# Ranking two of eight expert heads between the next stage's dot products instead of inside the query stage

## Chip, cores and metric

The kernel runs on one NeuronCore of a Trainium2 chip. The metric is the device time of one execution in microseconds (us); three runs of each kernel are timed.

## What is computed

One step of a one-layer decoder for a prompt of 512 tokens and a sample group of 8 x 8 tokens: a Mamba-2 branch, a sparse-attention branch, their merge, an output projection, and then a retrieval layer, which the change is about:

```python
def _peer(h, peer_wq, peer_sub_keys, peer_u, peer_v):
    n = h.shape[0]
    q = (h @ peer_wq).reshape(n, PEER_HEADS, 2, PEER_HALF)
    s = jnp.einsum('nhcd,hckd->nhck', q, peer_sub_keys).astype(jnp.float32)
    top_s, top_i = lax.top_k(s, PEER_TOPK)
    cand_s = (top_s[:, :, 0, :, None] + top_s[:, :, 1, None, :]).reshape(n, PEER_HEADS, -1)
    cand_i = (top_i[:, :, 0, :, None] * PEER_KEYS + top_i[:, :, 1, None, :]).reshape(n, PEER_HEADS, -1)
    best_s, best_pos = lax.top_k(cand_s, PEER_TOPK)
    experts = jnp.take_along_axis(cand_i, best_pos, axis=-1)
    g = jax.nn.softmax(best_s, axis=-1)
    act = jax.nn.gelu(jnp.einsum('nd,nhkd->nhk', h, peer_u[experts]).astype(jnp.float32))
    return jnp.einsum('nhk,nhkd->nd', (g * act).astype(peer_v.dtype), peer_v[experts])
```

There are 8 heads with 16 experts each, so every token picks 128 rows of peer_u and 128 rows of peer_v, 4 KB each, out of tables of 16,384 rows.

## The kernel before

The tokens are in five tiles: 0 to 3 are the prompt (128 tokens each), 4 is the sample group. The layer's first part runs in two groups: group a is tiles 0 and 1, group b is tiles 2 and 3 with the sample tokens. Each group goes through the stages conv, ssd, zgate, branch (one block together), kv, qk, cmp_prompt, attn_prompt, merge, out and query. Then come the sample group's own stages: sample_state, mix, branch, cmp, attn, branch, out and query, and at last `rest`.

The retrieval itself (class `Experts`) is laid through all stages from group b's conv on. `lay_out` writes one order of 1,152 **places**: a place "u" is one gather of 128 rows of peer_u (512 KB, an indirect DMA issued by GpSimd, `gather`) and the dot product on VectorE that uses them (`dot_u`), a place "v" is one gather of peer_v, and every four of them a sum on TensorE (`sum_v`). Tile 0's u places are 0 to 127, tile 1's begin at 128, tile 2's at 448. The gathers land in a ring of 14 slots (`NR`; one more from the state stage on). A gather waits until the slot's last reader is done, so it can be only some 14 places ahead of the dots. Each stage has a share of places (`k.share`: conv 60, ssd 28, zgate 56, branch 46, kv 22, qk 30, cmp_prompt 10, attn_prompt 100, ..., query 46, state 112) and calls `ex.dve(i)`, `ex.act(i)`, `ex.pe(i)`, `ex.pool(i)` at fixed points of its own program; each call emits what is due up to place `lo(i + 1)`. All engines work in program order, so an emitted step that waits holds up the stage's own work behind it on that engine.

A tile's experts must be named before its u gathers. **Ranking a head** takes three steps of VectorE: the 16 best of both score halves (`rank_halves`, `top16`), the 16 best of their 256 sums (`rank_sums`), and the experts' numbers (`mark_places`, then `name_marked` on GpSimd, inside the query stage; `name_experts`, all on VectorE, elsewhere). The query stage (`stage_query`) multiplies out scores for its group's two tiles and ranks all 8 heads of the first (tile 0 or 2) itself; at its end VectorE and ScalarE form the softmax (`shift_best`, Exp, `share_best`) and ScalarE copies names and weights (`stage_routes`), and the stage's barrier waits for that. The second tile's scores are stored to memory, and its heads are ranked between the dots of later stages: `load_scores` on GpSimd fetches one head's scores (128 KB), `rank_scores`, `rank_sums` and `name_head` run on VectorE at the 1st, 4th and 7th place after the head's start, `index_head` on ScalarE. The starts are in `rank_place`: for tile 1 places 20 + 30h, for tile 3 places 448 + 20 + 9h.

In group a's query stage ScalarE and TensorE also turn the next group's input (`Ahead`: `turn` is eight transposes of one tile, `spread` eight copies), after the loop over the 16 score halves. The state stage begins on GpSimd with masks and products of its own (L2129 to L2145), ahead of `ex.pool(0)`; on VectorE with `ex.dve(0)`, `ex.dve(1)`, and then the first update of a state (L2223), which waits for TensorE (L2173).

Of the kernel before, what the change touches and what calls it, by code (L numbers as in the profile page):

```python
# [6 lines left out]
F32 = mybir.dt.float32  # L7
# [1890 lines left out]
def stage_query(nc, k, g, following):  # L1898

    with ExitStack() as ctx:  # L1900
# [8 lines left out]
        (sk_in, projected, q_copied, scored, s_copied, ranked, own_s, shifted, exped, routed) = (  # L1909
            sem(n) for n in ("sk_in", "projected", "q_copied", "scored", "s_copied", "ranked", "own", "shifted", "exped",  # L1910
                             "routed"))
# [4 lines left out]
        ex = k.ex  # L1916
        ex.plan(HOOKS, k.share["query"])
# [5 lines left out]
        def _(sp):  # L1923
            def store(i):
                sp.wait_ge(s_copied, i + 1)
                sp.dma_start(k.scores_dram[t0][:, i, :], s[:, i % NS_BUF, 1, :]).then_inc(s_out[i % NS_BUF], 16)
# [5 lines left out]
            for i in range(NS_BUF):  # L1932
                sp.wait_ge(s_out[i], 16 * (HC // NS_BUF))

        @block.gpsimd
        def _(pool):
            own = Link(pool, pool_s)
            for i in range(HOOKS):
# [3 lines left out]
                if i >= 4 and i % 2 == 0:  # L1942
                    h = (i - 4) // 2
# [8 lines left out]
        def _(pe):  # L1952
# [21 lines left out]
            for i in range(HC + 1):  # L1974
# [5 lines left out]
                if i:  # L1980
                    score(i - 1)
            ex.pe(HC + 1)
            ex.pe(HC + 2)
            if ahead:
                for i in range(len(following.tiles)):
                    ahead.turn(i)

        @block.scalar
        def _(act):
# [28 lines left out]
            if ahead:  # L2018
                for i in range(len(following.tiles)):
                    ahead.spread(i)  # L2020
            ex.act(HC + 1)
            act.wait_ge(shifted, 1)
            a.activation(k.best[:], k.best[:], ACT.Exp).then_inc(exped, 1)
            ex.act(HC + 2)
            act.wait_ge(routed, 1)
            act.wait_ge(named, PH)
            ex.stage_routes(t0)
            act.wait_ge(ex.staged, t0 + 1)

        @block.vector  # L2030
        def _(dve):
            v = nc.vector
            own = Link(dve, own_s)
            for i in range(HC + 2):
# [7 lines left out]
                if i >= 2 and i % 2 == 0:  # L2042
                    h = i // 2 - 1
# [8 lines left out]
                if i >= 3 and i % 2 == 1:  # L2052
                    h = (i - 3) // 2
                    rank_sums(v, own, k, h)
                    mark_places(v, own, k, hit[:, h % 2]).then_inc(marked, 1)
            shift_best(v, own, k).then_inc(shifted, 1)
            dve.wait_ge(exped, 1)
            share_best(v, own, k).then_inc(routed, 1)
# [3 lines left out]
        if following:  # L2062
            k.w.start(following)

            @block.sync
            def _(sp):
                sp.wait_ge(projected, HC)
                k.w.feed(sp)

# [1265 lines left out]
class Experts:  # L3335
# [10 lines left out]
    indexed = [0, 2, S]  # L3346

    def __init__(self, nc, k, ctx, looped):
        self.nc, self.k, self.looped = nc, k, looped
# [903 lines left out]
```

## Time and profile before

| | us |
|---|---|
| median of 3 runs | 2729.2 (2728.67 to 2739.69) |
| the profiled execution | 2731.53 |
| its span in the profile | 2729.7 |
| busy: TensorE, VectorE, ScalarE, GpSimd | 2018.4, 1456.9, 673.6, 1478.6 |
| group a's query stage | 585.4 to 669.4 |
| group b's query stage | 1499.9 to 1610.6 |
| sample_state | 1610.6 to 1807.8 |

In rows of the profile PE is TensorE (PEld its weight loads), DVE VectorE, ACT ScalarE, POOL GpSimd and SP the engine that only issues DMAs. `a <- b` names what an instruction writes and reads; `[x <- y]` is idle time x of the engine before it, ended by y. The DMA share is the mean busy share of the core's 16 DMA engines. A dot is one `CUSTOM_DVE_ANT_0` of L3768, 1.22 us long, and the next starts 1.15 us after it.

### The profile page before, as it was taken

Reading aid. Unit: us, or ns where it says so; the run is one execution under the profiler, and the core shown is the slowest. Engines: PE = TensorE matmul, PEld = TensorE weight load, DVE = VectorE, ACT = ScalarE, POOL = GpSimd, SP = SyncE. Lnnn points to the kernel's source line nnn. Section 1 sums busy time; section 2 is a strip of 40 time slices with the busy share of each in tenths; the row PEclk is TensorE's granted clock in tenths of the full one; section 3 lists DMA queues with packets and bytes.
Section 4 is the critical chain, followed back from the end, with each engine's and each line's share of the span. In section 5 each row is a group of like instructions: output and inputs, shape, how many; then the busy total and the mean of one; then the engine's idle time right before and its main releaser. Section 6 shows DMA issues by size and latency. Waiting matters only on the chain. (4 is left out here: it accounts for less than half of the span.)

```text
span 2729.7 us, 31629 instructions
## 1 busy us (share of the span) xinstructions
PE 2018.4 (74%) x10995; PEld 1286.9 (47%) x10995; DVE 1456.9 (53%) x3506; ACT 673.6 (25%) x2035; POOL 1478.6 (54%) x1493
## 2 busy tenths in 40 slices
PE   8999989987977979989988946755267776655044
PEld 6888875655655656654444722322144443111010
DVE  3331013226897975457731568778686665106910
ACT  4441016313547320015531112321011110001000
POOL 1120000006556766656654777787867777567775
PEclk9899989988988999989989967886588987868577
DMA  5414344344895899889889979999999999999998
GB/s 181 169 62 140 129 179 186 134 164 168 302 345 190 323 391 400 326 339 331 333 328 398 347 250 374 411 394 341 398 343 412 409 411 402 402 401 402 409 409 326
DMA packets 209780, 843.32 MB, mean 309 GB/s; under 512 B 25752, under 2 KB 32728, under 8 KB 190104
## 3 DMA queue, kind: packets, MB, share of 16 engines
q0 software_dynamic: 170912, 644.95, 61.8%
q1 hardware_dynamic: 38712, 196.36, 19.3%
q8 instruction: 89, 1.46, 0.2%
q14 instruction: 67, 0.55, 0.1%
HBM read 821.80 MB, written 23.54 MB: 310 GB/s over the span
## 5 line engine op out<-in xcount | busy, mean ns | idle before, releaser
L3604 POOL DMA_INDIRECT e_ring<-in_peer_u,e_idx x523 | 615.2, 1176 | 300.1 <-DVE e_dot L3768 142.7
L3768 DVE CUSTOM_DVE_ANT_0 e_ring<-e_ring,e_h 128x1024 f32<-128x1024 f32 x523 | 631.5, 1243 | 68.7 <-PEq L1159 22.0
L3604 POOL DMA_INDIRECT e_ring<-in_peer_v,e_idxT x487 | 510.7, 1049 | 258.5 <-issue 132.4
L3671 PE MATMUL ps<-e_ring,e_wz 128*32 128x512 f32 x1948 | 316.8, 698 | 261.9 <-DMA e_ring<-in_peer_v,e_idxT 152.9
L3671 PEld LDWEIGHTS ps<-e_ring,e_wz 128*32 128x32 f32 x1948 | 66.9, 119 | 416.7 <-issue 405.5
L363 PE MATMUL ps<-hT_ahead,wb 128*128 128x320 f32 x384 | 110.6, 443 | 0.9 <-DMA wb<-in_weights 0.9
L363 PEld LDWEIGHTS ps<-hT_ahead,wb 128*128 128x128 f32 x384 | 72.9, 195 | 30.1 <-issue 2.7
L1815 POOL CAST ra_atf<-ra_at 128x32 f32<-128x32 uint32 x8 | 1.7, 211 | 149.7 <-DVE ra_hit L1808 149.7
L3812 DVE TENSOR_TENSOR e_x<-e_x,ps 128x512 f32<-128x512 f32 x10 | 6.4, 684 | 141.8 <-PE ps L3671 141.8
L1183 POOL MEMSET inda<- 128x256 f32 x1 | 0.3, 311 | 147.7 <-POOLq L4071 147.7
L3671 PE MATMUL ps<-ring_pair,e_wz 128*32 128x512 f32 x152 | 63.2, 730 | 17.2 <-DMA e_ring<-in_peer_v,e_idxT 11.3
L642 POOL TENSOR_TENSOR sa_xdt<-xnata,dt 128x512 f32<-128x512 f32 x8 | 8.3, 1042 | 116.3 <-ACT hT_ahead L509 99.3
L547 DVE SCALAR_TENSOR_TENSOR ca_acc<-ca_in,vcol,ca_acc 128x256 f32<-128x256 f32 x72 | 34.9, 485 | 61.0 <-ACT ca_acc L492 59.3
L1648 DVE TENSOR_REDUCE apb_nmax<-ps 128x2 f32<-128x768 f32 (+1 forms) x32 | 34.9, 1090 | 47.2 <-PE ps L1540 47.2
L2173 PE MATMUL ps<-ss_bsel,ss_xde 64*128 64x512 f32 x64 | 39.6, 701 | 22.9 <-DVE wb L2223 13.4
L897 PE MATMUL ps<-hT_ahead,wb 128*128 128x320 f32 x192 | 56.0, 446 | 0.0
L547 DVE SCALAR_TENSOR_TENSOR cb_acc<-cb_in,vcol,cb_acc 128x344 f32<-128x344 f32 x72 | 41.7, 579 | 24.3 <-ACT cb_acc L492 22.6
L3671 PE MATMUL ps<-ring_more,e_wz 128*32 128x512 f32 x76 | 45.4, 729 | 7.7 <-DMA e_ring<-in_peer_v,e_idxT 7.7
L363 PE MATMUL ps<-hTa,e_ring 128*128 128x256 f32 x224 | 50.6, 380 | 0.0
L2980 DVE COPY as_pT<-ps 128x512 f32<-128x512 f32 x40 | 26.9, 688 | 43.9 <-PE ps L2849 43.9
L753 ACT ACTIVATE zs<-ps,nacum 128x128 f32<-128x128 f32 x128 | 36.6, 374 | 49.2 <-PE ps L681 49.1
L3039 DVE MAX8 top<-sq_s 128x8 f32<-128x128 f32 x16 | 3.9, 285 | 81.9 <-ACT sq_s L3290 81.5
(778 smaller groups left out, 4610.4 us busy)
## 6 DMA issues: line engine op xcount, KB each, us to landing
wb<-in_weights SPq DMA_DIRECT2D x65, 1024.0 KB, 7.3
e_ring<-in_weights SPq DMA_DIRECT2D x36, 1024.0 KB, 4.9
wb<-in_late_weights SPq DMA_DIRECT2D x6, 2048.0 KB, 10.9
room<-in_late_weights SPq DMA_DIRECT2D x6, 2048.0 KB, 15.7
h<-in_weights SPq DMA_DIRECT2D x10, 1024.0 KB, 8.3
xs<-in_weights SPq DMA_DIRECT2D x9, 1024.0 KB, 7.9
e_ring<-in_peer_u,e_idx POOLq DMA_INDIRECT x523, 8.7
e_ring<-in_peer_v,e_idxT POOLq DMA_INDIRECT x487, 10.6
```

What stands on the lines that cost most here:

```text
L363: last = nc.tensor.matmul(k.ps[:, f % 2, 0:N], w[:, kk, c:c + P], k.hT[:, kk, 0:N], start=(kk == 0), stop=(kk == KD - 1))
L547: last = v.scalar_tensor_tensor(out=dst, in0=src, scalar=wc, in1=dst, op0=ALU.mult, op1=ALU.add)
L642: gp.tensor_tensor(v3(xdt), x3, by_head(k.dt[:, t0 + c, hs], P), ALU.mult).then_inc(xdt_done, 1)
L753: last = a.activation(MT[:, q % 4, j, :], k.ps[:, 1, j * P:j * P + P], ACT.Exp, bias=k.nacum[:, t0 + c, hh:hh + 1])
L897: last = mm(k.ps[:, f % 2, 0:N], w[:, kk, :], k.hT[:, kk, 0:N], start=(kk == 0), stop=(kk == KD - 1))
L1648: v.tensor_reduce(nmax[:, 2 * d:2 * d + 2], k.ps[:, 0:2, 0:width(d)], AX.X, ALU.max, negate=True).then_inc(maxed, 1)
L2173: mm(k.ps[:, 2 + q % 2, :], xde[:, f * P:f * P + P], bsel[:, j % 2, seqs(i), :].rearrange("p b n -> p (b n)"), start=True, stop=True).then ...
L2980: v.tensor_copy(pT[:, 4 * i:4 * i + 4, :], k.ps[:, n % 2, :].rearrange("p (q c) -> p q c", q=4)).then_inc(p_copied, 1)
L3604: nc.gpsimd.indirect_dma_start(out=self.room(place), out_offset=None, in_=k.peer_u if kind == "u" else k.peer_v, in_offset=off).then_inc(s ...
L3671: last = nc.tensor.matmul(k.ps[32 * b:32 * b + 32, self.SUMS + i, :], self.wz[:, at:at + 32], self.room(self.v_at[n])[:, 512 * i:512 * i + ...
L3768: v.tensor_tensor_reduce(uu, uu, self.h[:, tile % 2, :], 1.0, 0.0, ALU.mult, ALU.add, self.dot[:, tile % 2, t:t + 1]).then_inc(self.dotted, 1)
L3812: last = v.tensor_tensor(self.x1[:, c], self.x1[:, c], k.ps[:, self.SUMS + i, :], ALU.add)
```

## The change

Both query stages rank only heads 0 to 5 (`EARLY = 6`) and no longer form the softmax; the barrier waits for the six heads' names alone. Scores of heads 6 and 7 of the first tile are stored too. Those two heads become steps between dots: for tile 0 they start at places 16 and 44, for tile 2 at places 449 and 458. Tile 1's eight heads start at 76, 100, 124, 154, 184, 214, 244 and 274 (from 20, 50, ..., 230), tile 3's at 482 + 9h (from 468 + 9h). The softmax steps follow a tile's last head. The transposes of the next group's input move into the loop. In group a's query stage the wait for the stores comes behind the issue of the next group's first weights.

```diff
@@ class Experts
+    EARLY = 6
+        self.heads = [(t, h) for t in range(S) for h in range(0 if t % 2 else self.EARLY, PH)]
@@ stage_query, SyncE
-                sp.dma_start(k.scores_dram[t0][:, i, :], s[:, i % NS_BUF, 1, :]).then_inc(s_out[i % NS_BUF], 16)
+                sp.dma_start(k.scores_dram[t0 + 1][:, i, :], s[:, i % NS_BUF, 1, :]).then_inc(s_out[i % NS_BUF], 16)
+                if i in left:
+                    sp.dma_start(k.scores_dram[t0][:, i, :], s[:, i % NS_BUF, 0, :]).then_inc(s_out[i % NS_BUF], 16)
@@ stage_query, GpSimd (VectorE alike)
-                if i >= 4 and i % 2 == 0:
-                    h = (i - 4) // 2
+                h = (i - 4) // 2
+                if i % 2 == 0 and 0 <= h < EARLY:
@@ stage_query, TensorE
+                if ahead and 12 <= i < 12 + len(following.tiles):
+                    ahead.turn(i - 12)
             ex.pe(HC + 1)
             ex.pe(HC + 2)
-            if ahead:
-                for i in range(len(following.tiles)):
-                    ahead.turn(i)
@@ stage_query, ScalarE
+                if ahead and 13 <= i < 13 + len(following.tiles):
+                    ahead.spread(i - 13)
             ex.act(HC + 1)
-            act.wait_ge(shifted, 1)
-            a.activation(k.best[:], k.best[:], ACT.Exp).then_inc(exped, 1)
             ex.act(HC + 2)
-            act.wait_ge(routed, 1)
-            act.wait_ge(named, PH)
-            ex.stage_routes(t0)
-            act.wait_ge(ex.staged, t0 + 1)
+            act.wait_ge(named, EARLY)
+            ex.index_rest(t0)
+            act.wait_ge(ex.rest_named, t0 // 2 + 1)
@@ Experts.lay_out
+        for t in range(S):
+            heads = [h for tile, h in self.heads if tile == t]
+            for i, h in enumerate(heads):
+                at = lambda step: self.rank_place(t, i, step)
+                if i >= 2:
+                    load = self.rank_place(t, i - 2, 8)
+                else:
+                    load = 66 + i if t == 1 else self.rank_place(2, i, 8) if t == 3 else self.u_at[P * t]
+                put("pool", load, lambda t=t, h=h: self.load_scores(t, h))
+                put("dve", at(1), lambda t=t, h=h: self.rank_scores(t, h))
+                put("dve", at(4), lambda t=t, h=h: rank_sums(self.nc.vector, self.own, self.k, h))
+                put("dve", at(7), lambda t=t, h=h: self.name_head(h))
+                put("act", at(13 if t < 2 else 9), lambda t=t, h=h: self.index_head(t, h))
...
-    def rank_place(self, t, step):
-        if t == 0 and step >= 0:
-            return 20 + 30 * (step // 9) + step % 9
-        return self.u_at[P * t + 20 + step]
+    def rank_place(self, t, i, step):
+        if t == 0:
+            return 16 + 28 * i + step
+        if t == 1:
+            return 76 + 24 * min(i, 2) + 30 * max(i - 2, 0) + step
+        return self.u_at[P * 2 + (34 if t == 3 else 1) + 9 * i + step]
```

VectorE at the start of the state stage, before: the seventh dot (with the read-out of its sum), the first update, the eighth dot.

```order
L3768 ISA e_ring,e_dot<-e_ring,e_h 128x1024
L3768 ISA e_dot 128x1
L2223 TENSOR_TENSOR wb<-wb,ps 128x512
L3768 ISA e_ring,e_dot<-e_ring,e_h 128x1024
L3768 ISA e_dot 128x1
```

And after the change, from the stage's second dot on (`e_s` is the tile into which a head's scores are loaded):

```order
L3786 ISA e_ring,e_dot<-e_ring,e_h 128x1024
L3786 ISA e_dot 128x1
L3039 MAX top<-e_s 128x8 x2
L3042 MAX_INDEX at<-top,e_s 128x8 x2
L3046 MATCH_REPLACE e_s<-top,e_s 128x128 x2
L3039 MAX top<-e_s 128x8 x2
L3042 MAX_INDEX at<-top,e_s 128x8 x2
L3786 ISA e_ring,e_dot<-e_ring,e_h 128x1024
L3786 ISA e_dot 128x1
```

Seven dots stood ahead of the first update; now two dots, a head's scores, three dots, its sums and two dots do.

GpSimd at the same place, after the change: the last of the stage's own products, then the loads of two heads' scores, then the first gathers. Before, the first gather stood right behind the product.

```order
L2145 TENSOR_TENSOR ss_bsel<-Bs,same 64x1024
L3632 DMA e_s<-scores_scratch 128x256 x2
L3616 DMA ring_more<-in_peer_u,e_idx 128x1024
L3616 DMA e_ring<-in_peer_u,e_idx 128x1024 x7
L3632 DMA e_s<-scores_scratch 128x256
```

So VectorE's third dot of the stage is behind a load that GpSimd issues only after its own products.

VectorE in group b's cmp_prompt stage, after the change: from the stage's first dot to the copy L1455, for which TensorE waits. Before, three dots stood ahead of that copy and nothing else.

```order
L3786 ISA e_ring,e_dot<-e_ring,e_h 128x1024
L3786 ISA e_dot 128x1
L3039 MAX top<-e_s 128x8 x2
L3042 MAX_INDEX at<-top,e_s 128x8 x2
L3046 MATCH_REPLACE e_s<-top,e_s 128x128 x2
L3039 MAX top<-e_s 128x8 x2
L3042 MAX_INDEX at<-top,e_s 128x8 x2
L3786 ISA e_ring,e_dot<-e_ring,e_h 128x1024
L3786 ISA e_dot 128x1
L3786 ISA e_ring,e_dot<-e_ring,e_h 128x1024
L3786 ISA e_dot 128x1
L1455 COPY cpb_pT<-ps 128x256
```

The head's sums now stand ahead of the stage's two copies L1395, and its name behind them at the stage's end.

## Rows read from the trace of the kernel before

**Rows 1.** The page: busy time of each engine; DMA busy tenths in 40 slices
```profile
PE 2018.4 (74%) x10995; PEld 1286.9 (47%) x10995; DVE 1456.9 (53%) x3506; ACT 673.6 (25%) x2035; POOL 1478.6 (54%) x1493
...
DMA  5414344344895899889889979999999999999998
```

**Rows 2.** Windows: length, busy PE, PEld, DVE, ACT, POOL, clock, DMA share, GB/s
```profile
585.40:669.40 84.00, 66.97 (x344) 59.41 (x344) 57.23 (x251) 26.72 (x74) 40.59 (x82) 0.91 0.38 128
...
904.00:988.00 84.00, 78.67 (x317) 53.97 (x316) 77.68 (x162) 23.72 (x72) 68.26 (x50) 0.97 0.96 366
...
1202.40:1224.20 21.80, 15.29 (x80) 10.56 (x80) 14.11 (x46) 3.16 (x6) 11.30 (x13) 0.69 0.86 297
1224.20:1401.00 176.80, 156.32 (x960) 79.45 (x960) 122.56 (x245) 99.07 (x247) 107.29 (x98) 0.97 0.87 323
...
1610.60:1807.80 197.20, 126.11 (x608) 62.88 (x608) 160.82 (x376) 59.06 (x171) 153.36 (x131) 0.79 0.97 376
```

**Rows 3.** Timeline, first query stage ends: start, us, engine, line, operation
```profile
652.87 0.23 POOL L1825 TENSOR_TENSOR expert<-ra_pick,ra_hit 128x16 f32<-128x16 f32 x1
...
667.23 0.23 POOL L1825 TENSOR_TENSOR expert<-ra_pick,ra_hit 128x16 f32<-128x16 f32 x1
...
669.45 6.78 PE L386 MATMUL ps<-hT_ahead,wb 128*32 128x320 f32 x16 [15.52 <-PEq L4071]
```

**Rows 4.** Timeline of VectorE inside the q/k stage: one head between dots
```profile
1170.90 0.48 DVE L3039 MAX8 top<-e_s 128x8 f32<-128x128 f32 x2
...
1174.05 1.22 DVE L3768 CUSTOM_DVE_ANT_0 e_ring<-e_ring,e_h 128x1024 f32<-128x1024 f32 x1 [0.19 <-DVE at L3042]
...
1175.20 0.42 DVE L3059 TENSOR_TENSOR cand<-top 128x256 f32<-128x256 f32 x1
...
1177.71 0.42 DVE L3042 FIND_INDEX8 pos<-best,cand 128x8 uint32<-128x256 f32 x1
...
1181.44 0.18 DVE L3065 CAST atf<-at 128x32 f32<-128x32 uint32 x1
...
1184.69 1.23 DVE L3768 CUSTOM_DVE_ANT_0 e_ring<-e_ring,e_h 128x1024 f32<-128x1024 f32 x1 [0.19 <-DVE expert L3079]
```

**Rows 5.** Timeline, compressed-attention stage of the second group
```profile
1217.80 0.42 DVE L1455 COPY cpb_pT<-ps 128x256 f32<-128x256 f32 x1
...
1218.48 4.18 PEld L1387 LDWEIGHTS ps<-cpb_pT,zs 128*128 128x128 f32 x16 [1.66 <-DVE cpb_pT L1455]
```

**Rows 6.** VectorE waits, attention stage of group b: total us, times, longest
```profile
DVE apb_nmax L1648 <- PE ps L1540: 47.2, 26, 3.9
```

**Rows 7.** Timeline of GpSimd around the end of the second query stage
```profile
1584.21 0.23 POOL L1825 TENSOR_TENSOR expert<-rb_pick,rb_hit 128x16 f32<-128x16 f32 x1
...
1603.38 0.94 POOL L3604 DMA_INDIRECT e_ring<-in_peer_u,e_idx  x1 [0.30 <-issue]
...
1610.64 1.80 POOL L2129 MEMSET ss_cmask<- 128x2048 f32 x1 [1.95 <-POOLq L4071]
...
1628.86 1.02 POOL L3604 DMA_INDIRECT ring_more<-in_peer_u,e_idx  x1 [0.16 <-issue]
```

**Rows 8.** Score loads from memory (tile e_s), all of the span
```profile
DMA to landing us min/median/max: 4.5/8.1/12.8
```

**Rows 9.** Windows of L3604 alone from the first gather of the state stage
```profile
1628.80:1657.00 28.20, 21.75 (x18) 0.80 0.90 316
1628.80:1664.20 35.40, 27.43 (x23) 0.74 0.93 336
```

**Rows 10.** Timeline of VectorE, state stage: the first and the 17th dot
```profile
1610.80 1.22 DVE L3768 CUSTOM_DVE_ANT_0 e_ring<-e_ring,e_h 128x1024 f32<-128x1024 f32 x1 [15.22 <-PEq L4071]
...
1643.08 1.21 DVE L3768 CUSTOM_DVE_ANT_0 e_ring<-e_ring,e_h 128x1024 f32<-128x1024 f32 x1
```

**Rows 11.** Windows of the state stage from 1631 us, columns as above
```profile
1631.00:1700.00 69.00, 43.56 (x194) 23.20 (x193) 62.20 (x143) 20.13 (x58) 54.33 (x47) 0.75 0.98 362
1700.00:1808.00 108.00, 78.57 (x406) 37.62 (x407) 83.60 (x220) 35.53 (x103) 82.83 (x73) 0.86 1.03 411
```

More of the change, by code:

```diff
@@ L1916, in stage_query @@
         ex = k.ex
+        EARLY = ex.EARLY
+        left = range(2 * EARLY, HC)
+        assert 2 * EARLY >= HC - NS_BUF
+        stores = [sum(1 + (i in left) for i in range(HC) if i % NS_BUF == b) for b in range(NS_BUF)]
         ex.plan(HOOKS, k.share["query"])
@@ L1931, in _ @@
                 store(i)
-            for i in range(NS_BUF):
-                sp.wait_ge(s_out[i], 16 * (HC // NS_BUF))
+            if not following:
+                for i in range(NS_BUF):
+                    sp.wait_ge(s_out[i], 16 * stores[i])
         @block.gpsimd
@@ L2068, in _ @@
                 k.w.feed(sp)
+                for i in range(NS_BUF):
+                    sp.wait_ge(s_out[i], 16 * stores[i])
 def v_of(kv, branch, g):
@@ L3463, in lay_out @@
                 put("pool", end + 48, lambda t=t: self.load_x1(t + 1))
+        for t in range(S):
[11 more added lines that the diff above has]
+                put("act", at(13 if t < 2 else 9), lambda t=t, h=h: self.index_head(t, h))
+                assert at(13) + self.NR < self.u_at[P * t + TOPK * h]
+            end = lambda step: self.rank_place(t, len(heads) - 1, 9 + step)
+            exp, share, stage = (6, 12, 18) if t < 2 else (1, 5, 12)
+            put("dve", end(0), lambda: self.shift_all())
+            put("act", end(exp), lambda t=t: self.exp_best(t))
+            put("dve", end(share), lambda t=t: self.share_all(t))
+            put("act", end(stage), lambda t=t: self.stage_routes(t))
+            assert end(stage) < (self.rank_place(t + 1, 0, 1) if t % 2 == 0 else self.u_at[P * t + P - 1])
         put("pool", 0, lambda: self.load_x1(0))
@@ L3713, in index_first, with index_rest @@
         a.copy(self.idx[:, tile % 2, 0:TOPK], k.expert[:, 0, :]).then_inc(self.first_named, 1)
+    def index_rest(self, tile):
+        act, a, k = self.nc.scalar, self.nc.scalar, self.k
+        early = k.expert[:, 1:self.EARLY, :].rearrange("p h k -> p (h k)")
+        a.copy(self.idx[:, tile % 2, TOPK:TOPK * self.EARLY], early).then_inc(self.rest_named, 1)
     def index_head(self, tile, h):
@@ L3719, in index_head @@
             act.wait_ge(self.routed_v, tile - 1)
-        act.wait_ge(self.head_named, PH * self.looped.index(tile) + h + 1)
+        act.wait_ge(self.head_named, self.heads.index((tile, h)) + 1)
         a.copy(self.idx[:, tile % 2, TOPK * h:TOPK * h + TOPK], k.expert[:, h, :]).then_inc(self.head_indexed, 1)
@@ L3785, in rank_scores @@
         dve = self.nc.vector
-        count = self.looped.index(tile) * PH + h
+        count = self.heads.index((tile, h))
         dve.wait_ge(self.s_in[count % 2], 16 * (count // 2 + 1))
```

70 lines of the change are left out of this document (25 added, 45 removed).

## The prediction, made before the change was run

> **What bounds the kernel now.** I read the page first, then the windows by stage, then the timeline at the two ends of the query stages and where the moved heads land. No engine is full over the span: TensorE 74%, GpSimd 54%, VectorE 53% [rows 1]. The DMA engines, though, are at 80 to 90% of their time from the fourteenth slice on and at 90% or more from the 25th, which is about where the state stage begins [rows 1]. From there to the end the kernel is a stream of gathers: 411 GB/s at a share of 1.03 over 108 us of it [rows 11]. DMA time left idle there does not come back, and a later start of that stream is a later end.
>
> Ahead of it each stage has its own bound. In group a's query stage the DMA is at 0.38: the stage waits for engines [rows 2]. In group b's zgate TensorE has 78.7 and VectorE 77.7 of 84 us. In cmp_prompt nothing is full, it is a chain of waits. In attn_prompt TensorE has 156 of 177 us and VectorE waits 47.2 us for it in 26 pieces [rows 2, 6]. In the state stage DMA is at 0.97 and VectorE works 160.8 of 197.2 us [rows 2]. These are the places of the sum. It is made against the profiled execution's own 2731.5 us; the median of the three runs is 2.3 below that.
>
> **First boundary, group a's query stage.** The stage ends when GpSimd has named the last head, at 667.46; TensorE starts the next stage 2.0 us later. The sixth head's name is there at 653.10 [rows 3]. What remains for ScalarE by then is the last of the transposed input's copies, which the change moves into the loop, so that they are no new end. The gain is 667.46 - 653.10 = **14.4 us**. Doubled stores of the last four score halves could hold SyncE back by some 2 us, so its bounds are 12 and 14.4. The six gathers behind the name move with it. The scores and sums of two heads leave VectorE here at no cost or gain of their own.
>
> **What two heads cost elsewhere.** The q/k stage shows one between dots: scores from 1170.98 to 1174.05, sums from 1175.28 to 1178.13, names from 1181.52 to 1184.69, so 3.1 + 2.9 + 3.2 = 9.2 us of VectorE [rows 4]. Group b's stages up to the query stage get two heads more, and tile 1's move back. By shares of places:
>
> - conv has two heads before and after, ssd one and one: nothing but softmax steps of under 1 us.
> - zgate (places 88 to 143) had one head and the scores of another, now two whole ones: 6.1 us more on an engine that idles 6.3 of 84 us [rows 2]. But the scores that stood at its very end are gone, and the branch stage behind it starts with less in its way. I take +2, bounds -3 and +6.1.
> - kv and q/k lose or keep what they had; TensorE bounds them. Nothing.
> - cmp_prompt gets a whole head, the scores ahead of L1455, for which TensorE waits [rows 5], the sums ahead of the copies L1395, the names ahead of the barrier. TensorE sums for other places before L1455's reader and ends as the copy does, so the scores' 3.1 show in full; of sums and names I take half, 3: **+6**, bounds 3 and 9.2.
> - attn_prompt gets a whole head in three consecutive turns of its loop. A piece is about 3.1 us; VectorE's idle time in a turn is 47.2/26 = 1.8 on the average [rows 6]. What does not fit delays ScalarE and then TensorE: 3 x (3.1 - 1.3) = **+5.5**, bounds 0 and 9.2. I leave it 0.5 us less cover than the average, since the waits are uneven.
>
> Together +13.5, so that the first boundary is nearly spent by 1401 us.
>
> **Second boundary, group b's query stage.** The sixth name is done at 1584.4. Twelve gathers are left for GpSimd at 1.24 us each, until 1599.5; before, two heads' names stood between them and the last came at 1608.7 [rows 7]. Its products in the state stage took 18.2 us from 1610.64 to the first gather at 1628.86, of which 3.5 were a wait for a load that is now early enough. So that point (call it T) comes at 1599.5 + 14.7 = 1614.2, **14.7 us** sooner; at least 9.2 if only the names' time is saved.
>
> **The state stage.** Here the change adds a wait. VectorE's third dot is behind a head's scores, which GpSimd loads at T and no sooner. Before, VectorE made eight dots between the barrier and T; now two. A load takes 4.5 us at the least and 8.1 in the middle [rows 8]; few DMAs are under way at T, so I take 6. From T on VectorE then needs 6 for the load, 3.1 for scores, 15 dots to the 17th at 1.15, two sums, a name and another head's scores (12.1), and three updates at 0.6: 17th dot done at T + 40. Before it was done at 1644.3, T + 15.4 [rows 10]. With 14 slots and one more, the 18th gather from T waits for that dot. Before, it was issued at T + 28 [rows 9], so there are 12.6 us of slack and the lag is 12. For the 23rd, issued at T + 35.3 before, I get T + 51, a lag of 15; for later ones 8 to 12. Queued behind are ScalarE (it waits for names) and TensorE and the updates behind ScalarE. The DMA engines stand idle meanwhile, and behind 1700 us they are full [rows 11], so nothing is won back. **+12**, bounds 0 (the ring covers it) and 30: load 6, six dots 6.9 and two heads 18.4, less 1, none of it in VectorE's 31 us of idle time after 1631 [rows 11].
>
> The Trainium skill (DMA: Bandwidth & Descriptors, the fit of a DMA's duration) gives a fixed 2.0 us and the bytes at 436 GB/s, so 2.3 us for such a load. By it the load would land 3.7 us sooner than I take, this term would be 8.3, and the sum 3.7 us lower, with the same verdict. The rows have none under 4.5 us, and the sum goes by them.
>
> **Bytes.** Eight stores of 64 KB and four loads of 128 KB more, about 1 MB: 2.6 us at 411 GB/s, less than half of it where the DMA is full. +1, bounds 0 and 2.6.
>
> **The sum.** -14.4 + 2 + 6 + 5.5 - 14.7 + 12 + 1 = -2.6. 2731.5 - 2.6 = 2728.9, and for the median 2726.6: I forecast **2727 us, no change**. 0.5% (13.6 us) is about what a measurement of this kernel can tell from no change.
>
> **Rivals.**
>
> *The heads hide (faster).* If zgate costs nothing, cmp_prompt 3, attn_prompt 2, the state stage 3 and the bytes nothing, the sum is -29.1 + 8 = -21, the time **2708**. For it: VectorE is idle 54 of 177 us in attn_prompt and 31 after 1631 us. Against it: in cmp_prompt and at the start of the state stage the new work stands directly ahead of what others wait for, by the order of the program.
>
> *The state stage falls behind VectorE (slower).* The mechanism is the stall at the third dot. If the lag it starts is not taken up by the ring and by VectorE's idle time, but TensorE, ScalarE and VectorE wait in turns for updates that all begin late, it grows from 12 to the bound of 30: +18 on the sum, **2745**. It decides from a lag of about 28 us, where the total passes 13.6 above before. For it: the first update moves from 1630.9, T + 2, to about T + 18, and the stage's 32 updates are one chain. Against it: VectorE worked only 83.6 of the last 108 us [rows 11].
>
> *The first boundary does not open.* SyncE now has to see the doubled stores land after it has issued weights. If these share the DMA with them and take 5 us and more longer, the gain is 9 instead of 14.4: **2732**.
>
> **Chances.** The forecast's case 0.58, its own range 2716 to 2739; heads hidden 0.25; the slow state stage 0.11; the stores 0.06. With 2 in 100 of the forecast's case beyond its range on the fast side and 1 on the slow side, faster by over 0.5% is 0.27, slower 0.12, within 0.61. The range that leaves out 2 in 10 goes from 2706, just below the first rival, to 2742, short of the second.
>
> **What would show it.** In the profile after: TensorE's first instruction of group b's conv near 655 (14 sooner); cmp_prompt 25 to 31 us long (21.8 before) and attn_prompt 179 to 186 (176.8); the first score load of the state stage near T, 18 us before a first gather no longer stands free but behind it; a wait of VectorE of some 15 to 25 us for `e_s` after two dots; fewer gathers in T to T + 35 than the 23 of before, about 14; the state stage's length some 15 us more from its barrier. I am wrong if attn_prompt and cmp_prompt keep their length, if the DMA share of the first 70 us after T stays at 0.9 in spite of the stall, or if the state stage is longer by more than 25 us from T on.

## The result, and the profile after the change

| | us |
|---|---|
| the kernel before, five runs | median 2736.5 (2728.67 to 2739.69) |
| the change, five runs | median 2754.25 (2749.11 to 2759.25) |
| ratio, 95% interval | 1.0072 (1.0049 to 1.0094) |
| profiled execution of the change, its span | 2749.11, 2747.4 |

The change is slower by 0.7%, 17.7 us between the two profiled spans. I had forecast 2727 and a range up to 2742: both were wrong. (Two more runs had moved the median of the kernel before from 2729.2 to 2736.5. Moved by as much, the range would end at 2749, and 2754 is still outside.)

The page after the change, busy time and DMA tenths, against [rows 1]:

```profile
PE 2053.6 (75%) x10995; PEld 1305.6 (48%) x10995; DVE 1456.1 (53%) x3526; ACT 675.9 (25%) x2040; POOL 1458.5 (53%) x1461
...
DMA  5414444446895999888889989999999999999998
```

VectorE's total is the same within 1 us (heads moved, none was added). The bytes are 844.4 MB after 843.3, the 1 MB more that I had counted. TensorE is busy 35 us longer with the same instructions, at a mean granted clock of 0.861 instead of 0.870. What differs otherwise is where work stands. Windows of the change by stage (length, busy PE, PEld, DVE, ACT, POOL, clock, DMA share, GB/s): group a's query, group b's conv, zgate, cmp_prompt, attn_prompt, then sample_state and sample_branch; four of them answer to [rows 2] (the window of zgate runs on into branch here, so it does not):

```profile
583.80:658.10 74.30, 67.13 (x344) 59.53 (x344) 42.44 (x186) 24.45 (x70) 36.23 (x68) 0.96 0.45 149
658.10:810.20 152.10, 127.69 (x548) 87.56 (x548) 127.57 (x276) 72.76 (x279) 73.32 (x64) 0.92 0.87 310
904.80:1009.40 104.60, 94.43 (x387) 66.04 (x386) 89.45 (x202) 27.57 (x79) 73.86 (x58) 0.95 0.99 382
1201.60:1230.40 28.80, 16.88 (x78) 11.75 (x78) 22.53 (x81) 3.16 (x6) 13.52 (x14) 0.68 0.77 261
1230.50:1411.30 180.80, 159.02 (x960) 81.36 (x960) 131.07 (x280) 99.25 (x248) 106.80 (x96) 0.96 0.84 310
1603.60:1823.70 220.10, 138.69 (x608) 69.44 (x608) 163.03 (x407) 60.76 (x176) 156.03 (x139) 0.73 0.95 364
1905.90:1961.30 55.40, 21.15 (x68) 6.62 (x68) 53.57 (x121) 2.98 (x7) 39.08 (x31) 0.65 0.94 340
```

Two windows that the rows ahead did not show, of the kernel before: group b's conv and sample_branch.

```profile
669.40:815.40 146.00, 126.55 (x548) 86.67 (x548) 124.25 (x268) 69.56 (x275) 77.69 (x70) 0.93 0.91 325
1891.70:1941.10 49.40, 19.40 (x68) 6.07 (x68) 43.08 (x74) 1.08 (x3) 40.54 (x32) 0.71 0.93 353
```

From the last instruction of one stage to that of the next, the difference of the two traces runs so (the change began group a's query stage 1.6 us earlier, which the change does not explain):

| stretch | before | after | difference | sum so far |
|---|---|---|---|---|
| up to group a's query | | | -1.6 | -1.6 |
| group a's query | 84.0 | 74.0 | -10.0 | -11.6 |
| group b's conv | 146.7 | 153.1 | +6.4 | -5.2 |
| ssd | 92.9 | 94.6 | +1.7 | -3.5 |
| zgate, branch | 196.6 | 199.3 | +2.7 | -0.8 |
| kv, q/k | 97.5 | 97.5 | 0 | -0.8 |
| cmp_prompt | 21.7 | 28.8 | +7.1 | +6.3 |
| attn_prompt | 176.9 | 180.9 | +4.0 | +10.3 |
| merge, out | 98.2 | 100.0 | +1.8 | +12.1 |
| query b to T, GpSimd's first gather of the state stage | 129.7 | 115.5 | -14.2 | -2.1 |
| T to the end of sample_state | 178.9 | 196.9 | +18.0 | +15.9 |
| everything behind | 921.9 | 923.7 | +1.8 | +17.7 |

So the first boundary was spent before kv began, and the state stage took back more than the second gave.

**One thing told ahead of the prediction was misread.** Tile 3's starts, "468 + 9h" and "482 + 9h", are not places. `rank_place` looks the number up in tile 2's dots, and from the 28th dot on four dots alternate with four gathers of peer_v. They are tile 2's dots 20 + 9h and 34 + 9h. Tile 3's last head therefore starts not at place 545, in the state stage, but well behind it. Before, it stood in the mix stage. After, it is at 1915 us, in sample_branch. VectorE there, after:

```profile
1915.17 0.48 DVE L3039 MAX8 top<-e_s 128x8 f32<-128x128 f32 x2
...
1921.77 0.42 DVE L3059 TENSOR_TENSOR cand<-top 128x256 f32<-128x256 f32 x1
...
1928.18 0.18 DVE L3065 CAST atf<-at 128x32 f32<-128x32 uint32 x1
```

**The first boundary, after.** GpSimd, SyncE's queue, ScalarE and TensorE where the stage ends, against [rows 3]:

```profile
651.17 0.23 POOL L1825 TENSOR_TENSOR expert<-ra_pick,ra_hit 128x16 f32<-128x16 f32 x1
651.55 1.02 POOL L3616 DMA_INDIRECT e_ring<-in_peer_u,e_idx  x1 [0.15 <-issue]
...
657.84 0.94 POOL L3616 DMA_INDIRECT e_ring<-in_peer_u,e_idx  x1 [0.31 <-issue]
...
652.65 0.32 SPq L1929 DMA_DIRECT2D scores_scratch<-ra_s  x1
653.01 0.43 SPq L1931 DMA_DIRECT2D scores_scratch<-ra_s  x1
653.49 1.00 SPq L4002 DMA_DIRECT2D wb<-in_weights  x2
...
652.19 0.43 ACT L2002 COPY ra_s<-ps 128x256 f32<-128x256 f32 x1
652.44 0.34 ACT L3731 CAST e_idx<-expert 128x80 uint32<-128x80 f32 x1
...
660.14 7.24 PE L386 MATMUL ps<-hT_ahead,wb 128*32 128x320 f32 x16 [9.12 <-DMA wb<-in_weights]
```

The sixth name is there at 651.40, as predicted (the start is 1.6 us earlier). But the barrier opens at 658.1. The last two stores of scores are issued at 652.65 and 653.01, behind the copy that the early transposes pushed back to 652.19, and beside six gathers. The view of their tile gives the six stores before them and these two:

```profile
DMA to landing us min/median/max: 1.6/1.7/1.7
...
DMA to landing us min/median/max: 3.6/3.6/3.6
```

They land at 656.6, 5.2 us behind the sixth name, and the barrier opens 1.5 us later. TensorE does not start with it, though. Its wait is ended by the first weights, which SyncE issues at 653.49, behind the stores and beside the gathers, 6.7 us ahead of TensorE's start. Before, they were issued at 652.29 and landed at 654.76. So TensorE starts 2.0 us behind the barrier, and an earlier barrier alone would not have started it sooner.

**The state stage, after.** GpSimd and VectorE at its start, against [rows 7, 10]; and the windows of the gathers from T on, against [rows 9]:

```profile
1612.29 0.94 POOL L3616 DMA_INDIRECT e_ring<-in_peer_u,e_idx  x1 [0.30 <-issue]
1613.22 1.83 POOL L2129 MEMSET ss_cmask<- 128x2048 f32 x1
...
1625.33 1.21 POOL L3632 DMA_DIRECT2D e_s<-scores_scratch  x2
1626.83 1.03 POOL L3616 DMA_INDIRECT ring_more<-in_peer_u,e_idx  x1 [0.30 <-issue]
...
1631.38 0.49 DVE L3039 MAX8 top<-e_s 128x8 f32<-128x128 f32 x2 [25.26 <-DMA e_s<-scores_scratch]
...
1643.24 0.68 DVE L2223 TENSOR_TENSOR wb<-wb,ps 128x512 f32<-128x512 f32 x1
```

```profile
1626.80:1654.80 28.00, 15.11 (x12) 0.62 0.76 253
1626.80:1662.10 35.30, 18.66 (x15) 0.65 0.77 265
```

VectorE waits 25.3 us behind two dots. In 35.3 us GpSimd issues 15 gathers where it had issued 23, and the DMA engines work 0.77 of the time instead of 0.93.

How the lag goes on, from T in both traces: the 18th gather is issued 12.3 us late, the 23rd 15.7, the 57th 16.3, and the last of the stage (the 109th) 11.8. The 20th to the 30th of the stage's 32 updates are 13.5 to 14.5 us late, the last two 18. VectorE between the 30th update and these two, before and then after the change:

```profile
1797.54 0.69 DVE L2223 TENSOR_TENSOR room<-room,ps 128x512 f32<-128x512 f32 x1 [1.97 <-PE ps L2173]
...
1799.29 0.42 DVE L3059 TENSOR_TENSOR cand<-top 128x256 f32<-128x256 f32 x1
...
1805.69 1.28 DVE L2223 TENSOR_TENSOR room<-room,ps 128x512 f32<-128x512 f32 x2
```

```profile
1810.03 0.69 DVE L2223 TENSOR_TENSOR room<-room,ps 128x512 f32<-128x512 f32 x1 [1.97 <-PE ps L2173]
1810.64 0.17 DVE L3065 CAST atf<-at 128x32 f32<-128x32 uint32 x1
...
1817.33 0.48 DVE L3039 MAX8 top<-e_s 128x8 f32<-128x128 f32 x2
...
1821.64 1.28 DVE L2223 TENSOR_TENSOR room<-room,ps 128x512 f32<-128x512 f32 x2
```

Before, the sums of a head of tile 3 stood there (3.0 us). After, by the later starts, a name and another head's scores do (6.4 us). That is the step from 14.5 to 18.

TensorE's 608 instructions of the stage took 138.7 us instead of 126.1, at a granted clock of 0.73 instead of 0.79. In `second_sync` below, without the long stall, it is 135.2 us at 0.73, and in `none`, in the same set and without the two heads, 129.6 at 0.77. What that costs the stage was not separated.

### The profile page after: what moved, and what is told of

It reads as the page before. It is cut to its first block and busy times, and to the rows that moved or that the text cites. A ratio compares the mean times of both kernels' runs of the same rounds, so it can differ in the third digit from the quotient of the medians.

```text
span 2747.4 us, 31637 instructions
## 1 busy us (share of the span) xinstructions
PE 2053.6 (75%) x10995; PEld 1305.6 (48%) x10995; DVE 1456.1 (53%) x3526; ACT 675.9 (25%) x2040; POOL 1458.5 (53%) x1461
## 5 line engine op out<-in xcount | busy, mean ns | idle before, releaser
L3616 POOL DMA_INDIRECT e_ring<-in_peer_v,e_idxT x487 | 503.1, 1033 | 271.9 <-issue 134.7
L3683 PE MATMUL ps<-e_ring,e_wz 128*32 128x512 f32 x1948 | 324.9, 712 | 253.1 <-DMA e_ring<-in_peer_v,e_idxT 141.6
L3683 PE MATMUL ps<-ring_pair,e_wz 128*32 128x512 f32 x152 | 65.6, 758 | 17.1 <-DMA e_ring<-in_peer_v,e_idxT 10.3
L2180 PEld LDWEIGHTS ps<-ss_h0t,ss_cmask 128*64 128x64 f32 x256 | 34.3, 164 | 39.5 <-ACT ss_h0t L2203 20.1
L2180 PE MATMUL ps<-ss_h0t,ss_cmask 128*64 128x128 f32 x256 | 43.7, 326 | 8.9 <-ACT ss_h0t L2203 4.8
## 6 DMA issues: line engine op xcount, KB each, us to landing
e_ring<-in_peer_v,e_idxT POOLq DMA_INDIRECT x487, 10.2
```

The costliest lines, as they stand in the source:

```text
L2180: last = mm(k.ps[0:NS, 5, fj * P:fj * P + P], cmask[:, j, HB * i + b, :], h0t[:, q % 2, b, :], start=(i == 0 and b == 0), stop=(i == 1 and ...
L3616: nc.gpsimd.indirect_dma_start(out=self.room(place), out_offset=None, in_=k.peer_u if kind == "u" else k.peer_v, in_offset=off).then_inc(s ...
L3683: last = nc.tensor.matmul(k.ps[32 * b:32 * b + 32, self.SUMS + i, :], self.wz[:, at:at + 32], self.room(self.v_at[n])[:, 512 * i:512 * i + ...
```

## The experiments

All compare with the kernel before, run in the same set. In the four sets it took 2812.8, 2798.1, 2737.6 and 2738.6 us (medians), and in the first two attn_prompt and attn_sample are longer in every kernel. So ratios are compared across sets, stage lengths within one. How far a ratio can be trusted shows in `none`, below, which I expected at 1.000 and which came out at 1.0028. Effects under 0.3% are read from stage lengths alone. These come from one execution of each kernel, which can lie 10 us and more off the median (`combined` 16 above, `none` 17 below), so a few us in one stage count only where several traces repeat them.

**Set 1: the loads, and each boundary alone**

`a_sync`, in the state stage (and a semaphore of their own for these loads):

```diff
+            for h in range(PH - 2, PH):
+                sp.dma_start(ex.s[:, h % 2], k.scores_dram[2][:, 2 * h:2 * h + 2, :]).then_inc(ex.s_early[h % 2], 16)
```

> The change with one thing altered: the scores of tile 2's heads 6 and 7 are fetched by SyncE at the start of the state stage, not by GpSimd behind its own products. Theory A (the stall of VectorE at its third dot is what the state stage lost): the wait of 25.3 us for e_s is under 5 us, the first update comes before 1630 instead of 1643, the stage from GpSimd's first gather behind the products to its end takes about 180 us instead of 196.9 (178.9 in the kernel before), and the whole is about 16 us shorter than the change, 2738 against 2754. Theory B (two heads' 18.4 us of VectorE are the loss, wherever they stand): the stall goes, the stage stays within 5 us of the change's 220 us, and the whole is 2750 or more.

`a_gpsimd`:

```diff
+            for h in range(PH - 2, PH):
+                ex.load_scores(2, h)
             gp.memset(cmask[:], 0.0).then_inc(cleared, 1)
```

> The change with GpSimd's two loads of scores ahead of its own products in the state stage, not behind them: about 12 us earlier (1613 instead of 1625), still behind the ten gathers it issues first. Theory A: VectorE's wait falls from 25.3 to about 13 us, the stage is 9 to 12 us shorter, the whole about 2744. Theory B: as the change, 2750 or more. Theory C (a lag below some 15 us is covered by the ring of 14 slots): as good as the loads by SyncE.

Measured: 1.0043 (1.0017 to 1.007) and 1.0085 (1.0054 to 1.0116). VectorE's wait is 7.3 us in the first and 25.7 in the second:

```profile
DVE top L3041 <- DMA e_s<-scores_scratch: 7.3, 1, 7.3
```

```profile
1630.20 0.94 POOL L3619 DMA_INDIRECT e_ring<-in_peer_u,e_idx  x1 [0.30 <-issue]
1631.14 1.22 POOL L3635 DMA_DIRECT2D e_s<-scores_scratch  x2
...
1649.73 0.49 DVE L3041 MAX8 top<-e_s 128x8 f32<-128x128 f32 x2 [25.71 <-DMA e_s<-scores_scratch]
```

SyncE's loads, issued at 1618.7, were there after 9 us (`a_sync` waits for them until 1627.9). GpSimd's, issued at 1631.1 right behind its gathers, took 18.6 us, though they stood 13.5 us ahead of the first gather of the stage. From query b's start to the state stage's end the change took 311.7 us; here it is 296.9 with SyncE's loads, 314.9 with GpSimd's. Within the set, it is 312.3 with the change's late loads (`second_only`, below) and 312.7 with no head of tile 2 in the stage (`first_only`). So theory A holds for the stage: without the stall the second boundary's gain is there, some 15 us. It does not hold for the whole. I expected 16 us less than the change; the ratio fell from 1.0072 to 1.0043, with intervals that overlap, and `first_only` without any second boundary is as fast (1.0039). The comparison within the set is `a_sync` with `a_gpsimd`: 2826.4 and 2838.6 us. My theory of the second run was wrong: behind a queue full of gathers, an earlier issue is worth nothing.

`second_only` (tile 0 ranks eight heads, tile 1's at 20 + 30h) and `first_only` (tile 2 ranks eight, tile 3's at dots 20 + 9h): in both, `EARLY` per tile, and the kernel before's softmax at the end of the stage that ranks eight.

> Only group b's query stage ranks six heads (tile 2), tile 0 ranks eight inside its stage and tile 1's heads stand where they stood before; the early transposes stay. If the parts add up as the two traces say (query stage b 19 us shorter to its barrier, the state stage's end 15.9 later less the 12.1 that came from ahead): about 4 us over the kernel before, 2737 to 2743 beside 2736. If the loss sits in the state stage alone, the whole loss of 18 us shows here.

> Only group a's query stage ranks six heads (tile 0), with tile 1's heads at the 76th place and on; tile 2 ranks eight inside its stage and tile 3's heads start at 468 + 9h as before. If the parts add up: query stage b begins 12 us later than before and the whole is about 12 us over the kernel before, 2748. The theory of the prediction (first boundary and moved heads cancel, -14.4 + 13.5) gives no difference, 2736.

Measured: 1.0058 (1.0033 to 1.0083) and 1.0039 (1.0013 to 1.0065). Together they would make 1.0097, which their intervals do not part from the whole's 1.0072. `first_only` is what the parts said (12 us) and not what the prediction's theory said (nothing). `second_only` is 16 us over the kernel before where the parts had said 4. Neither boundary paid alone.

**Set 2: where the heads stand**

`none` (both tiles rank eight, all places as before), `places` (the same with tile 1's starts of the change), `second_sync` (`second_only` with SyncE's loads), and `combined`, the change with SyncE's loads and:

```diff
-            return 76 + 24 * min(i, 2) + 30 * max(i - 2, 0) + step
+            return [72, 88, 112, 146, 162, 178, 194, 212][i] + step
```

> The change's code with all eight heads of tiles 0 and 2 ranked inside the query stages and all other heads at the places of the kernel before: only the early transposes and the later wait for the stores are left of the change. Every theory expects no difference from the kernel before (within 0.2%); its trace is the measure for the others of this call. If it is slower by some us, part of the loss is in neither the heads nor the stall.

> As none, but tile 1's eight heads at the places of the change (76, 100, 124, 154, 184, 214, 244, 274 instead of 20 + 30h). Theory of the places (the moved heads cost 6 us in cmp_prompt, 4 to 9 in attn_prompt and something in zgate): cmp_prompt 29 us instead of 23, attn_prompt 4 to 9 us longer, in all 10 to 20 us slower than none, ratio 1.004 to 1.007. Rival: the places cost 6 us in cmp_prompt alone, and the loss of the first part comes from the shortened stage itself (gathers and weights that now collide): ratio 1.002.

> As none, but tile 2 ranks six heads in its query stage, and the two others' scores are fetched by SyncE at the start of the state stage. From the run that moved these loads in the whole change (query b and state stage together 297 us, against 312 in the others): 12 to 16 us faster than none, ratio to the kernel before 0.994 to 0.997. If the gain of the second boundary is eaten later by the full DMA, no difference.

> The change with SyncE's loads and with tile 1's heads at places 72, 88, 112, 146, 162, 178, 194 and 212: one less in zgate's second half (none at places 124 to 131, where tile 0's weights are formed), none in cmp_prompt or attn_prompt, three in kv and q/k, where VectorE idles half the time. If those three places were the cost: cmp_prompt back to 23 us, attn_prompt as in none, the first part 5 to 10 us shorter than in none, and the whole 18 to 25 us faster than none, ratio 0.991 to 0.994. If the first part gains nothing even so: as second_sync.

Measured: 1.0028 (1.0008 to 1.0047), 1.0014 (0.9997 to 1.0031), 1.0004 (0.9986 to 1.0023) and 1.0012 (0.9989 to 1.0034). No ratio came out as expected: `none` is above its 0.2%, `places` is no slower than `none`, and the gains of `second_sync` and above all of `combined` (18 to 25 us) are not there.

That `none` is slower leaves a rival: the early transposes and the later wait for the stores could cost something themselves. Its trace shows none of it where they stand. Group a's query stage takes 84.1 us (84.0 before), and from there to kv it is 435.9 (436.2). Whether they cost anything behind that stays open.

Last instruction to last instruction, in us:

| | none | places | second_sync | combined |
|---|---|---|---|---|
| conv of group b | 146.8 | 131.7 | 147.1 | 152.5 |
| ssd, zgate, branch | 289.1 | 297.5 | 287.8 | 294.7 |
| cmp_prompt | 22.1 | 29.4 | 22.1 | 22.0 |
| attn_prompt | 187.4 | 193.1 | 189.3 | 192.9 |
| query b and state | 309.2 | 309.9 | 299.1 | 305.3 |

The surprise is conv. Windows of none and of places, conv alone:

```profile
665.30:811.40 146.10, 126.63 (x548) 86.74 (x548) 124.27 (x268) 69.59 (x276) 77.75 (x70) 0.93 0.92 325
```

```profile
667.50:798.40 130.90, 124.46 (x548) 85.68 (x548) 110.73 (x204) 68.75 (x275) 76.55 (x66) 0.97 0.95 350
```

Without two heads VectorE is busy 13.5 us less and the stage is 15.2 shorter: in conv nearly all of VectorE's time is the stage's. Two later traces without heads there have the same 131.7. Part of it only moves: ssd to branch is 8.4 longer in `places`. The head in cmp_prompt costs 7.3 us, and is gone from `combined`; over all traces the stage is 21.7 to 23.2 us long without it and 28.8 to 29.5 with it. `combined`'s attn_prompt is as long as that of `places` though no head stands in it; in this set I cannot say what sets it.

**Set 3: a version from these findings**

`tile3_dense` (the change with tile 3's heads 7 dots apart), `places_free` (`none` with tile 1's starts below), `best` (the two together with SyncE's loads, tile 0 ranking eight heads, tile 2 six), `stores_first`:

```diff
+        if t == 1:
+            return [76, 100, 118, 150, 168, 186, 200, 218][i] + step
+        return self.u_at[P * 2 + (34 + 7 * i if t == 3 else 1 + 9 * i) + step]
@@ stores_first, SyncE
+                for i in range(NS_BUF):
+                    sp.wait_ge(s_out[i], 16 * stores[i])
                 sp.wait_ge(projected, HC)
                 k.w.feed(sp)
-                for i in range(NS_BUF):
-                    sp.wait_ge(s_out[i], 16 * stores[i])
```

> The change with tile 3's heads started at its 34th, 41st, 48th ... dot (7 apart) instead of 34 + 9h; the last starts at the 83rd dot, as in the kernel before, not at the 97th. The traces show the last of them at 1915 to 1928 us in the change, inside the sample_branch stage, which takes 55.4 us in every run with the later starts and 46.5 to 49.4 in those with the earlier. Theory L (the late head lengthens that stage): sample_branch 47 to 49 us instead of 55.4, the whole 5 to 8 us under the change. Rival (the stages from the state stage on are one stream of gathers, and a stage's length only divides it): sample_branch shorter, the next stages longer by as much, the whole as the change.

> As none (eight heads ranked inside both query stages), with tile 1's heads at places 76, 100, 118, 150, 168, 186, 200 and 218: none in group b's conv, which VectorE bounds (111 of 133 us busy without heads), none in cmp_prompt or attn_prompt. From the runs with the change's places: conv 132 us instead of 147, ssd and zgate together 8 longer; then, if heads in cmp_prompt and attn_prompt were the cost there, cmp_prompt 22 us and attn_prompt as in none, and the whole 7 us under the kernel before, ratio 0.9975. If attn_prompt is 5 us longer all the same, it is not the heads that lengthen it, and the ratio is 1.000.

> places_free, and tile 2 ranking six heads with SyncE's loads, and tile 3's heads 7 dots apart. If the three gains add up: 7 from the places, 10 at the second boundary, 6 in sample_branch, so 23 us under the kernel before, ratio 0.992. If the stream of gathers bounds everything behind the state stage, only what comes ahead of it counts and the ratio is 0.995 to 1.000.

> The change with SyncE waiting for the stores of scores ahead of the issue of the next weights in group a's query stage (the order of the kernel before). In the change the last two stores land 3.6 us after issue, beside gathers and weights, and the barrier stands 1.5 us behind them. Theory: the stores land in 1.7 us, the barrier comes 2 us sooner, the weights are issued 1 to 3 us later and TensorE begins no sooner than now (660); the whole as the change within 3 us. If the barrier stays where it is, another engine sets it.

Measured: 1.0103 (1.0073 to 1.0134), 0.9992 (0.9973 to 1.0011), **0.9941 (0.9918 to 0.9963)** and 1.0074 (1.0049 to 1.01).

- `tile3_dense`: sample_branch fell from 55.4 to 48.1 us, as theory L had it, but the state stage rose to 227.5 and mix to 85.8. From the state stage to sample_branch it is 361.4 us against 358.4 in the change. So denser heads only moved the load. That is the rival's outcome, though not its way: the time came back in the stages ahead, where the heads now stand closer, and not behind. The late head's place alone is not what was lost.
- `places_free`: conv 131.7, cmp_prompt 21.8, attn_prompt 177.4 (before 176.9). So here attn_prompt follows its heads: 176.9 to 177.6 us in four traces without one, 180.1 to 182.3 in four with one. The gain, 6 us at the end of q/k (the earlier start taken off), shrank to 4 by the state stage's end and cannot be told from nothing in the ratio.
- `best` is faster than both kernels, 0.6% under the one before (I expected 0.8%), and 0.5% faster than `places_free` in the same set. It keeps only the second boundary: tile 0 ranks all eight heads in its stage. The two profiled executions show the gain over `places_free` up to the state stage's end (10.2 us, with a start 2 us later) and then no more (0.3 us where attn_sample begins, 2.3 at the end), so they do not show where the medians' 13 us arise. Its load waits in the state stage are 8.6 us, and query b and state together 296.0 us (308.6 before):

```profile
DVE top L3051 <- DMA e_s<-scores_scratch: 8.6, 1, 8.6
```

```profile
1587.30:1791.60 204.30, 128.29 (x608) 64.54 (x608) 171.38 (x442) 61.16 (x177) 157.93 (x138) 0.76 1.01 392
```

- `stores_first`: the stores still took 3.5 to 3.8 us with no weights under way, so it is the gathers that slow them. The last instruction of the stage came at 658.3 instead of 657.1: SyncE now waits and then issues. My 2 us sooner was wrong. The weights, issued at 656.99, landed at 662.44, and TensorE began at 662.49: it is their landing that it waits for.

**Set 4: the first boundary once more**

`spread_late` moves ScalarE's copies of the turned input one step on; `best_first` is `best` with tile 0 ranking six heads, and these copies as in `spread_late`.

```diff
-                if ahead and 13 <= i < 13 + len(following.tiles):
-                    ahead.spread(i - 13)
+                if ahead and 14 <= i < 14 + len(following.tiles):
+                    ahead.spread(i - 14)
```

> The change with the copies of the turned input one step later in ScalarE's loop, so that the copy of the last scores (which the last two stores wait for) stands ahead of the last eight of them: it is done at about 651.4 instead of 652.6. Theory S (the landing of the last stores sets the first barrier): these are issued at 651.4 to 651.8, ahead of most of the gathers, land between 653 and 655.5, and the stage's last instruction is at 655 or 656 instead of 657.1. Rival G (GpSimd's gathers behind the sixth name, until 658.8, set it): it stays at 657. The whole as the change, within 4 us either way.

> The best version (0.9941 of the kernel before) with tile 0, too, ranking only six heads in its query stage, its two others in conv at places 16 and 44, and the copies of the turned input as in spread_late. Conv without heads takes 131.7 us, with two heads 153: if the first boundary's 10 to 12 us are less than what the two heads and their softmax cost in conv (21), this is 8 to 12 us slower than the best version, ratio 0.997 to 0.999. If the heads' places behind conv win it back, 0.992 to 0.995.

Measured: 1.0103 (1.0072 to 1.0134) and 0.9992 (0.997 to 1.0013). The edit of `spread_late` did not do what it was made for: TensorE's loop ended 3.7 us later (654.7 against 651.0), since the copies now stood ahead of what it waits for, and the last stores were issued at 656.8 and 657.1. Yet it tells theory S from rival G. These stores took up to 5.6 us and landed by 662.7, and the stage's last instruction is at 663.3. GpSimd, on the other hand, was through with its gathers 3.7 us before it could go on:

```profile
DMA to landing us min/median/max: 4.3/5.0/5.6
```

```profile
660.12 0.94 POOL L3616 DMA_INDIRECT e_ring<-in_peer_u,e_idx  x1 [0.30 <-issue]
664.76 1.18 POOL L3632 DMA_DIRECT2D e_s<-scores_scratch  x2 [3.71 <-POOLq L4089]
```

So the landing of the last stores sets this barrier: it opens 1.5 us behind it here (664.3) as in the change (658.1). In `best_first` conv took 150.5 us against 131.7 in `best`, and it lost the whole 0.5%. Some 6 of these 14 us are the flaw of the late copies (the query stage took 80.4, not 74.0).

## Why the prediction was wrong, by its steps

The sum was -2.6 where the profiled spans differ by 17.7. Step by step:

- **First boundary, -14.4: measured -10.0, and -7.7 to TensorE's first instruction** (both less the earlier start). The step that failed is the "some 2 us" for SyncE's doubled stores. They took 3.6 us instead of 1.6, and an instruction that the change moved (the copy behind the early transposes) made them later. The rival of the stores, at chance 0.06 and a gain of 9, had the landing right, but laid it to the weights; it is the gathers. The weights' own landing, at which TensorE starts, was in no term.
- **Conv, "nothing": measured +6.4.** This is the step that went most astray, since I never read conv's row: VectorE was busy 124.25 of 146.0 us there, in short pieces of one chain. VectorE is busy 3.3 us more after the change: one dot more (1.3), the rest of the second head's name, which had fallen behind conv's end (1.4), and the first softmax steps (0.5). With 2.3 us of TensorE's later start (7.7 against 10.0) that makes 5.6 of the 6.4, if the two add up, which no run tests. With it goes the larger error: I treated two heads in conv as paid for. They cost 15 us there (`none` against `places`, of which 8 come back behind conv), so that a boundary worth 8 to 10 us can win little by leaving two heads over as long as they go to conv.
- **zgate and branch, +2: measured +2.7; ssd, nothing: +1.7.** The first is inside its bounds; the second had no term and is not explained.
- **cmp_prompt, +6: measured +7.1; attn_prompt, +5.5: +4.0.** The way of costing (what stands ahead of the instruction that others wait for) was right, and `none` against `places` shows the first alone, +7.3. Merge and out gave +1.8 where I had nothing; not explained.
- **Second boundary, -14.7: measured -14.2.** Right: the two names saved and the wait for a load gone, as summed.
- **State stage, +12, bounds 0 and 30: measured +18.0.** The mechanism was right in each piece: load 6 us (6.0 to 6.3), wait 25.3 (I had said 15 to 25), first update at T + 16.4 (T + 18), 15 gathers in 35 us (14). The gathers' lags came as said too, at the start and at the end: 12.3 at the 18th (12), 15.7 at the 23rd (15), up to 16 in the middle and 11.8 at the last (8 to 12). The step that failed is taking the 12 us of the gathers for the loss of the stage. The stage ends with its updates. They were 14.5 us late, and the last two another 3.5, by the head work that tile 3's later starts put ahead of them. I had no term for that, and had those starts at the wrong places. The slow rival, at 0.11, had the updates late, but its lag that grows from 12 to 30 did not come.
- **Bytes, +1:** not measured apart; everything behind the state stage gave +1.8.

Of the signs, cmp_prompt, attn_prompt and the gathers behind T came as said. TensorE's start did not: 660.1 where I had said near 655.

By an estimate from the fit of the Trainium skill (DMA: Bandwidth & Descriptors, anatomy of one DMA) that load would have landed in 2.3 us and the term been 8.3. The trace had 6.0, and the stage lost 18: the rows decided, and they should have.

The chances were wrong in kind too. The forecast leant on two large gains, the first at its best bound and the second with no term for less, and took the state stage well below the middle of its bounds; slower by over 0.5% had 0.12. That a chain-bound stage without a row in the argument stood between gain and end should have moved it up.

## What to carry to other kernels

A barrier that opens sooner is worth what the next stage can use. Before work is moved out of a stage, read the row of every stage that it is moved into, and above all of the one that is costed at nothing. A short load that the critical engine waits for belongs on another engine's DMA queue than the stream of gathers, and at the stage's start. Here that, with tile 1's heads put where VectorE idles, tile 3's closer together and group a's query stage left at eight heads, gave a kernel 0.6% faster than the one before, where the change lost 0.7%. Which of these gives how much was not separated: `second_sync`, with the loads alone, could not be told from the kernel before.

## What the runs showed of the hardware

- A load of 128 KB issued by GpSimd behind its own indirect gathers of 512 KB landed 18.6 us after issue; the same load from SyncE, with the gathers still under way, after 9 us; from GpSimd once the gathers had been issued 13 us before, after 6.0. The Trainium skill (DMA: Bandwidth & Descriptors, queues, rings and completion order) says that a DMA engine takes turns between queues packet by packet, and the 9 us agree: the load did not wait for all of the gathers ahead. The Trainium skill (Trainium Kernel Development and Optimization, key constraints) says that issuing from several engines at once only saves issue time. Here the load from SyncE was issued 9 us earlier in the stage, and it also landed 9 us faster; the median of the kernel was 12 us lower.
- A store of 64 KB lands in 1.6 to 1.8 us with little else under way, in 3.6 beside the six gathers, and in up to 5.6 where it is issued later among them. In the kernel before, three in a row took 4.9 to 6.0 us earlier in the same stage, beside and right behind its first eight gathers (626.6 to 635.4).
- A dot that runs beside one of GpSimd's two products in the state stage (L2131, L2133) takes 4.3 to 4.6 us instead of 1.22: two before the change (1616.5 and 1621.1), none after it, since VectorE stood still there, and again two in `a_sync` and one in `best`. So moving the loads to SyncE does not bring all of the stall back.
- The kernel before took 2812.8 us (median) in one set and 2737.6 in another, at mean granted clocks of 0.853 and 0.865 over its executions, and both are noted with the same chip number, 5. What makes the difference is open. Up to group a's query stage the traces of all kernels agree within some 5 us; the difference comes in attn_prompt (177 to 182 against 187 to 198, heads in it or not) and attn_sample (297 to 302 against 317 to 338), where the gathers run.
